# Gate blocks transposed by VectorE in 32x32 squares, and a convolution moved behind the rotation

## The chip, the cores and the metric

One core of a Trainium2 chip runs the whole program. The metric is device time in microseconds for one execution; lower is better.

## The reference

A trunk of two layers on 256 tokens of width 2048, in float32. Layer 0 computes retention and a gated linear recurrence (RG-LRU) side by side from one input projection; layer 1 is sliding-window attention; a squared-ReLU MLP of width 8192 follows each. What the change touches is the recurrent block:

```
q, k, v, g, xb, gate = split(h @ w_in)
xc = conv_b + sum over taps of xp[:, tap:tap+S] * conv_w[tap]      # 4 taps along the tokens
r = sigmoid(xc @ w_a + b_a);  i = sigmoid(xc @ w_x + b_x)          # per block of 128 channels
a = exp(-8 r softplus(-lam));  b = sqrt(1 - a^2) * i * xc
h = scan(a, b);  lru_out = h * gelu(gate)                          # tanh form of gelu
q, k = rotary(q), rotary(k)                                        # for the retention part
```

## The kernel before, in words

The kernel streams weights. Each projection is cut into **blocks** of 512 output columns; there are 89 of them, and each has a **slot** (numbered from 0) on TensorE. Slots 0 to 11 are the blocks of `MIX_IN`: xb, gate, q, k, v, g for the first half of the channels, then the same for the second. A slot is eight **halves**, k = 0 to 7. Each half multiplies 256 rows of weights with 256 tokens. A float32 product is made from three: each operand is split into a high part and a low part, so a half is 12 matmuls (lines 1127 to 1129).

ScalarE writes the high part of a half's weights (`cut_hi`, line 579), VectorE subtracts to get the low part (`cut_lo`, line 788). Both work four halves ahead (`AHEAD`), in a ring of four (`RING`), so at step k of slot b they cut half k + 4. TensorE starts a half when its low part is there, and ScalarE may cut into a ring place when TensorE has left it. SyncE loads 1 MB of weights as soon as two halves of the unit that lay in its place are cut.

Each engine runs the same double loop over slots and steps. In every step VectorE does, in this order: what block b - 1 needs (`post`), the retention's step, the recurrent block's steps (`lru`), the attention's step, and last the cut. An instruction waits on the engine for its semaphores, and everything written behind it waits too.

What `post` does for a finished block b - 1 in slot b: ScalarE scales it out of PSUM to `stage` at step 0 (`leave`, line 629). An xb block is transposed by VectorE in 16 instructions of 32x256 (`turn_quadrants`, line 983), spread over steps 1, 2 and 3 by `QUADRANTS_AT`. A gate block is transposed by TensorE in eight matmuls with the identity (`turn_block`, line 1158) after half 2, and copied from PSUM to `gate_t` by VectorE at step 3 (line 1031). A q or k block is rotated by VectorE at step 1 (`rotate`, lines 833 to 838), transposed by TensorE after half 4, and copied at step 5.

The recurrent block has eight channel groups n = 0 to 7. `LRU_IN_SLOT` gives them slots 2, 3, 4, 5, 8, 9, 10 and 11; `lru(n, step)` runs with step = k in that slot, and step = 8 + k in the next. VectorE makes the convolution at step 2 (line 865 and three times line 868), TensorE the gate matmuls after half 4 (`lru_gates`, lines 1191 and 1192, behind a wait on `conv_done`), ScalarE the sigmoids, exponential, tanh and root at steps 5 to 7, and VectorE the scan at step 8. At step 9 ScalarE writes the high part of h and VectorE the low part (line 893). TensorE waits for these low parts in slot 12 (`LRU_BEFORE`). GpSimd computes the polynomial and product of gelu (lines 553 to 557), once the gate block is transposed and the group before is done. In slot 1, at step 6, VectorE also runs the softplus of the decay parameters, 14 small instructions.

Of the kernel before, what the change touches and what calls it, by code (L numbers as in the profile page):

```python
# [45 lines left out]
LG = LRU_BLOCKS // 2  # L46
TAPS = 4
# [22 lines left out]
def mlp_blocks(last_kind):  # L70
    blocks = []
    for c in range(CHUNKS):
# [15 lines left out]
NORM_OF = [0] * MIX_OUT0 + [None] * COLS + [1] * 32 + [2] * (1 + KV) + [None] * COLS + [3] * 32  # L88
BY_ACT = {"xb", "gate", "q", "k", "v", "g", "kv", "aq", "up"}
TURNED = {"xb", "gate", "q", "k", "g", "kv", "aq", "up", "res"}  # L90
DIRECT = {"xb", "kv"}
BY_QUADRANT = {"up", "res"} | DIRECT
SPLIT = {"g", "up", "res"}
PLAIN = TURNED - SPLIT - DIRECT
FROM_STAGE = {"gate", "aq"}

TURN_AT = {"aq": 0, "q": 4, "k": 4, "g": 4, "gate": 2}

QUADRANTS_AT = {kind: {1: 4, 2: 6, 3: 6} for kind in BY_QUADRANT}
STATIONARY_STARTS = ({MIX_OUT0, MLP0, QKV0, ATT_OUT0, MLP1}  # L100
                     | {m + PERIOD * c + COLS for m in (MLP0, MLP1) for c in range(CHUNKS)})

# [16 lines left out]
def late(b):  # L119


    return 2 if b in WOVEN else 0
# [3 lines left out]


LRU_BEFORE = {2: 4, 4: 6, 5: 8}


def lru_steps(b, k):
# [7 lines left out]
def total(kinds, each):  # L139

    out = [0]
    for kind, _ in BLOCKS:
        out.append(out[-1] + (each if kind in kinds else 0))
    return out
# [7 lines left out]
N_TURNED = total(TURNED, 2)  # L152
N_MOVED = total(TURNED - DIRECT, 2)
N_SPLIT = total(SPLIT, 2)


def out_at(kind, b):

    return (max(QUADRANTS_AT[kind]) if kind in BY_QUADRANT else TURN_AT[kind]) + 1 + late(b)

# [66 lines left out]
def build(nc, t):  # L227
    ctx = ExitStack()
    with ctx:
# [33 lines left out]
        def take(*shape):  # L263
            n = int(np.prod(shape))
            at = place["at"]
            place["at"] = at + n
            assert place["at"] <= AREA, (place["at"], AREA)
            v = area[:, at:at + n]
            if len(shape) == 2:
                v = v.rearrange("p (a b) -> p a b", a=shape[0])  # L270
            if len(shape) == 3:
                v = v.rearrange("p (a b c) -> p a b c", a=shape[0], b=shape[1])
            return v
# [3 lines left out]
        xb_t = take(LG, TAPS - 1 + SEQ)  # L277
        gate_t = take(LG, SEQ)
        q_t = take(HG, SEQ)
        k_t = take(HG, SEQ)  # L280
# [15 lines left out]
        kk_t = take(KV, SEQ)  # L296
        qq_t = take(PAIRS, SEQ)
# [96 lines left out]
        def vec(c):  # L394
            return vecs[:, c:c + 1]
# [170 lines left out]
        def _(act):  # L566
# [39 lines left out]
            def leave(slot, kind, j):  # L606

                b = slot.b - 1
                act.wait_ge(half_used, slot.halves(late(b)))
                if b > 0 and BLOCKS[b - 1][0] in DIRECT:  # L610

# [161 lines left out]
        def _(dve):  # L773
            links = [0]

            def link(ins):

                links[0] += 1
                ins.then_inc(chain, 1)
                dve.wait_ge(chain, links[0])  # L780
# [79 lines left out]

            def lru(n, step):
                xb = xb_t[:, n % LG, :]
                if step == 2:

                    link(nc.vector.tensor_scalar(xc[:, :], xb[:, 0:SEQ], vec(V_CONV + n), vec(V_CB + n),
                                                 ALU.mult, ALU.add))
                    for tap in range(1, TAPS):
                        ins = nc.vector.scalar_tensor_tensor(  # L868
                            xc[:, :], xb[:, tap:tap + SEQ], vec(V_CONV + LRU_BLOCKS * tap + n), xc[:, :],
                            ALU.mult, ALU.add)  # L870
                        if tap < TAPS - 1:
                            link(ins)
                    ins.then_inc(conv_done, 1)
                if step == 6:

                    dve.wait_ge(th_done, n + 1)
                    nc.vector.tensor_scalar(th[:, :], th[:, :], 2.0 ** -116, None, ALU.max).then_inc(th_safe, 1)
                if step == 8:

                    dve.wait_ge(sig_done, 2 * n + 2)  # L880
                    link(nc.vector.tensor_tensor(xc[:, :], xc[:, :], ri[:, 1, :], ALU.mult))
                    dve.wait_ge(root_done, n + 1)
                    link(nc.vector.scalar_tensor_tensor(th[:, :], a_lru[:, :], 1.0, th[:, :], ALU.add, ALU.mult))
                    link(nc.vector.memset(th[:, 0:1], 1.0))
                    link(nc.vector.tensor_tensor(xc[:, :], xc[:, :], th[:, :], ALU.mult))
                    if n > 0:
                        dve.wait_ge(lru_hi, n)
                    link(nc.vector.tensor_tensor_scan(h_lru[:, :], a_lru[:, :], xc[:, :], 0.0, ALU.mult, ALU.add))
                    dve.wait_ge(gelu_done, n + 1)
                    nc.vector.tensor_tensor(h_lru[:, :], h_lru[:, :], gel2[:, :], ALU.mult).then_inc(lru_done, 1)  # L890
                if step == 9:
                    dve.wait_ge(lru_hi, n + 1)
                    nc.vector.tensor_tensor(b_lo[:, 8 + n, :], h_lru[:, :], b_hi[:, 8 + n, :].bitcast(F32),
                                            ALU.subtract).then_inc(lru_lo, 1)
# [63 lines left out]
            def turn_quadrants(slot, k, kind, j):  # L958


                at = {tick + late(slot.b - 1): n for tick, n in QUADRANTS_AT[kind].items()}
                if k not in at:
                    return
                if k == min(at):

                    dve.wait_ge(turned_out, slot.count(N_TURNED, -1, INIT_HALVES))
                if k == min(at) and kind == "up":
                    dve.wait_ge(squared, slot.count(N_SQUARED, 0))
                if k == min(at) and kind == "res":
                    dve.wait_ge(evac_dve, slot.count(N_EVAC_DVE, 0))  # L970
                if k == min(at) and kind in DIRECT:
                    dve.wait_ge(evac_act, slot.count(N_EVAC_ACT, 0))
                src = x[:, :, j * NB:(j + 1) * NB] if kind == "res" else stage
                src = src.rearrange("p t (k f c) -> p t k f c", k=COLS, f=QUADRANTS)
                if kind in DIRECT:
                    tile = {"xb": xb_t[:, :, TAPS - 1:], "kv": kk_t}[kind]
                    dst = tile.rearrange("p k (t a c) -> p t k a c", t=TT, a=QUADRANTS)
                else:
                    dst = turn.rearrange("p m (k t a c) -> p t (m k) a c", k=2, t=TT, a=QUADRANTS)
                done = sum(n for tick, n in at.items() if tick < k)  # L980
                for n in range(done, done + at[k]):
                    a, f = divmod(n, QUADRANTS)
                    ins = nc.vector.transpose(dst[f * QUAD:(f + 1) * QUAD, :, :, a, :],  # L983
                                              src[a * QUAD:(a + 1) * QUAD, :, :, f, :])
                if k == max(at):
                    ins.then_inc(turned_out if kind in DIRECT else turned, 2)

            def plain_target(kind, j):
                tile = {"gate": gate_t, "q": q_t, "k": k_t, "aq": qq_t}[kind]
                return lambda m: tile[:, 2 * m:2 * m + 2, :]  # L990

            def post(slot, k):
# [28 lines left out]
                if kind in BY_QUADRANT:  # L1021
                    turn_quadrants(slot, k, kind, j)
# [91 lines left out]
        def _(pe):  # L1114
# [48 lines left out]
            def post(slot):  # L1163
# [3 lines left out]
                if kind not in TURNED - BY_QUADRANT:  # L1167
                    return
                if kind in FROM_STAGE:
                    pe.wait_ge(evac_act, slot.count(N_EVAC_ACT, 0))  # L1170
# [122 lines left out]
            def body(slot):  # L1293
                b = slot.b
                if b >= 2:
# [3 lines left out]
                    else:  # L1299
                        pe.wait_ge(evac_dve, slot.count(N_EVAC_DVE, -1))  # L1300
                if b in STATIONARY_STARTS:
                    pe.wait_ge(turned_out, slot.count(N_TURNED, -1, INIT_HALVES))
                for k in range(HALVES):
                    if b == 0:
                        pe.wait_ge(turned_out, k + 1)
                    if b == MIX_OUT0 and k in LRU_BEFORE:
                        pe.wait_ge(lru_lo, LRU_BEFORE[k])
                    if b == ATT_OUT0 and k == 0:
# [3 lines left out]
                    if b in WOVEN and k == HALVES - 2:  # L1312
# [3 lines left out]
                        else:  # L1316
                            pe.wait_ge(evac_dve, slot.count(N_EVAC_DVE, 0))
                    if b - 1 in STATIONARY_STARTS and k == 0:
                        pe.wait_ge(turned_out, slot.count(N_TURNED, -1, INIT_HALVES))
# [19 lines left out]
                    if b > 0:  # L1339
                        kind, j = BLOCKS[b - 1]  # L1340
                        if kind in TURN_AT and k == TURN_AT[kind] + late(b - 1):
                            post(slot)
# [33 lines left out]
```

## Time and profile before

| | us |
|---|---|
| median of 3 runs (2016.01 to 2016.54) | 2016.15 |
| the profiled execution | 2016.07 |
| its span, first to last instruction | 2014.3 |
| TensorE matmul busy | 2003.6 |
| VectorE busy | 1438.7 |
| ScalarE busy | 1019.9 |
| GpSimd busy | 45.2 |

The span belongs to the profiled execution; the rest of its 2016.07 us lies outside the first and the last instruction. PE is TensorE's matmul, PEld its weight load, DVE is VectorE, ACT is ScalarE, POOL is GpSimd. A matmul is listed at some 0.39 us though the next starts 0.23 us after it, since they are pipelined: differences of start times give the pace.

### The profile page before, as it was taken

The numbers are of one execution on the slowest core, as the hardware profiler recorded it, in microseconds if no ns is written. First come the engines' busy times: TensorE is split into PE (matmuls) and PEld (weight loads), VectorE is DVE, ScalarE is ACT, GpSimd is POOL, SyncE is SP. The second block draws the span as 40 slices with busy tenths as digits, with TensorE's granted clock in tenths as the row PEclk, the third lists the DMA queues.
The fourth block names the chain that finished last, engine by engine and source line by source line (L and its number), as shares of the span: only waits on it lengthen the run. The fifth ranks groups of instructions, "written<-read, shape, count | busy, mean of one in ns | idle before, by whom it ended". The sixth has DMA issues, their size and how long they took to land.

```text
span 2014.3 us, 24679 instructions
## 1 busy us (share of the span) xinstructions
PE 2003.6 (99%) x9187; PEld 1655.2 (82%) x9187; DVE 1438.7 (71%) x1975; ACT 1019.9 (51%) x1345; POOL 45.2 (2%) x55
## 2 busy tenths in 40 slices
PE   9999999999999999999999999999999999999998
PEld 7888888888888888888888877888888888888886
DVE  6777778987558657846888777978548756854875
ACT  6665665455345435434545555555435434544554
POOL 1110110000000000000000000000000000000000
PEclk9999999999999999999999999999999999999999
DMA  8556556556566656565656535566565656565563
GB/s 303 186 170 213 169 167 209 189 187 210 189 188 197 199 188 189 197 197 176 202 187 200 174 129 167 186 193 202 192 191 190 202 188 187 187 208 188 188 202 112
DMA packets 191437, 382.50 MB, mean 190 GB/s; under 512 B 6264, under 2 KB 7040, under 8 KB 191232
## 3 DMA queue, kind: packets, MB, share of 16 engines
q1 hardware_dynamic: 190112, 377.58, 57.7%
q0 software_dynamic: 1216, 3.88, 0.6%
q8 instruction: 49, 0.80, 0.2%
q14 instruction: 28, 0.23, 0.0%
q10 hardware_dynamic: 32, 0.01, 0.0%
HBM read 379.34 MB, written 2.10 MB: 189 GB/s over the span
## 4 chain that ended last, share of the span: by engine, by line
PE 95%; DVE 3%; ACT 2%; issue 0%; ACTq 0%
PE acc L1127 31%; PE acc L1129 30%; PE acc L1128 30%; ACT w_hi L579 1%; DVE w_lo L788 1%; PE bank L1158 0%; PE bank L1237 0%; PE bank L1261 0%; PE bank L1247 0%; DVE area L868 0%; PE acc L1278 0%; ACT L648 0%; ACT L654 0%; DVE turn L835 0%; PE bank L1191 0%
## 5 line engine op out<-in xcount | busy, mean ns | idle before, releaser
L788 DVE TENSOR_TENSOR w_lo<-raw,w_hi 128x1024 fp32r<-128x1024 f32 x712 | 865.5, 1225 | 520.2 <-ACT w_hi L579 517.4
L579 ACT ACTIVATE w_hi<-raw 128x1024 fp32r<-128x1024 f32 x712 | 748.1, 1059 | 809.0 <-PE acc L1129 805.6
L1127 PE MATMUL acc<-w_hi,a_hi 128*128 128x512 f32 x1568 | 614.6, 392 | 0.0
L1129 PE MATMUL acc<-w_hi,a_lo 128*128 128x512 f32 x1568 | 610.4, 389 | 0.0
L1128 PE MATMUL acc<-w_lo,a_hi 128*128 128x512 f32 x1568 | 610.3, 389 | 0.0
L1127 PE MATMUL acc<-w_hi,b_hi 128*128 128x512 f32 x1264 | 492.4, 390 | 0.0
L1129 PE MATMUL acc<-w_hi,b_lo 128*128 128x512 f32 x1264 | 491.8, 389 | 0.0
L1128 PE MATMUL acc<-w_lo,b_hi 128*128 128x512 f32 x1264 | 491.8, 389 | 0.0
L1127 PEld LDWEIGHTS acc<-w_hi,a_hi 128*128 128x128 f32 x1568 | 294.4, 188 | 62.6 <-issue 1.8
L1129 PEld LDWEIGHTS acc<-w_hi,a_lo 128*128 128x128 f32 x1568 | 294.3, 188 | 61.7
L1128 PEld LDWEIGHTS acc<-w_lo,a_hi 128*128 128x128 f32 x1568 | 294.4, 188 | 60.2
L1127 PEld LDWEIGHTS acc<-w_hi,b_hi 128*128 128x128 f32 x1264 | 237.2, 188 | 49.7 <-issue 0.7
L1129 PEld LDWEIGHTS acc<-w_hi,b_lo 128*128 128x128 f32 x1264 | 237.2, 188 | 49.4
L1128 PEld LDWEIGHTS acc<-w_lo,b_hi 128*128 128x128 f32 x1264 | 237.3, 188 | 49.2
L983 DVE STREAM_TRANSPOSE turn<-stage 32x256 f32<-32x256 f32 x512 | 223.1, 436 | 7.7
L587 ACT ACTIVATE b_hi<-turn 128x512 fp32r<-128x512 f32 x64 | 36.9, 625 | 107.2 <-DVE turn L983 107.2
L983 DVE STREAM_TRANSPOSE turn<-x 32x256 f32<-32x256 f32 x192 | 83.6, 436 | 2.9
L629 ACT ACTIVATE stage<-acc,rinv 128x512 f32<-128x512 f32 x92 | 57.6, 674 | 1.4 <-DVE rinv L821 1.4
L1001 DVE TENSOR_TENSOR x<-x,acc 128x512 f32<-128x512 f32 x78 | 49.8, 681 | 0.0
L796 DVE TENSOR_TENSOR b_lo<-turn,b_hi 128x512 fp32r<-128x512 f32 x64 | 41.2, 685 | 0.0
L634 ACT ACTIVATE stage<-stage 128x512 f32<-128x512 f32 x64 | 36.7, 626 | 0.0
L589 ACT ACTIVATE a_hi<-turn,vecs 128x256 fp32r<-128x256 f32 x24 | 12.1, 503 | 35.7 <-DVE turn L983 35.7
(171 smaller groups left out, 587.1 us busy)
## 6 DMA issues: line engine op xcount, KB each, us to landing
raw<-in_mlp_w_up SPq DMA_DIRECT2D x128, 1024.0 KB, 5.5
raw<-in_mlp_w_down SPq DMA_DIRECT2D x128, 1024.0 KB, 5.1
raw<-in_hyb_w_in SPq DMA_DIRECT2D x44, 1024.0 KB, 5.2
raw<-in_attn_w_qkv SPq DMA_DIRECT2D x20, 1024.0 KB, 5.1
raw<-in_hyb_w_out SPq DMA_DIRECT2D x16, 1024.0 KB, 5.2
raw<-in_attn_w_out SPq DMA_DIRECT2D x16, 1024.0 KB, 5.1
raw<-in_hyb_w_in SPq DMA_DIRECT2D x8, 512.0 KB, 9.9
out_y<-x SPq DMA_DIRECT2D x4, 512.0 KB, 3.0
```

The source lines that it names most:

```text
L579: nc.scalar.activation(w_hi[:, h % RING], raw[:, h // 2, 2 * (h % 2):2 * (h % 2) + 2, :], ACT.Copy).then_inc(hi_ready, 1)
L587: nc.scalar.activation(hi[:, kt:kt + 2, :], src, ACT.Copy).then_inc(turned_hi, 1)
L589: nc.scalar.activation(hi[:, kt, :], src[:, 0, :], ACT.Copy, scale=vec(scale))
L629: ins = nc.scalar.activation(stage[:, tt, :], src, ACT.Relu if kind == "up" else ACT.Copy, scale=s)
L634: nc.scalar.activation(stage[:, tt, :], stage[:, tt, :], ACT.Square).then_inc(squared, 1)
L788: nc.vector.tensor_tensor(w_lo[:, h % RING], raw[:, h // 2, 2 * (h % 2):2 * (h % 2) + 2, :], w_hi[:, h % RING].bitcast(F32), ALU.subtract) ...
L796: nc.vector.tensor_tensor(lo[:, kt:kt + 2, :], src, hi[:, kt:kt + 2, :].bitcast(F32), ALU.subtract).then_inc(turned_out, 1)
L983: ins = nc.vector.transpose(dst[f * QUAD:(f + 1) * QUAD, :, :, a, :], src[a * QUAD:(a + 1) * QUAD, :, :, f, :])
L1001: nc.vector.tensor_tensor(xs, xs, acc[:, b % 2, tt, :], ALU.add).then_inc(evac_dve, 1)
L1127: nc.tensor.matmul(a, xh, wh, start=first, stop=False)
L1128: nc.tensor.matmul(a, xh, wl, start=False, stop=False)
L1129: ins = nc.tensor.matmul(a, xl, wh, start=False, stop=last)
```

## The change

Gate blocks join the blocks that VectorE transposes straight to their place (`DIRECT`): six transposes at step 0 and ten at step 1 of the slot. TensorE's transposes and VectorE's copies for them go. The convolution runs at step `CONV_AT[n % 4]`: at step 1 for n = 1, 2, 5 and 6 (the slots of q and k, behind the rotation), and at step 2 for the others, as before. The low part of h is written at step 10 in place of step 9.

```
-DIRECT = {"xb", "kv"}
+DIRECT = {"xb", "kv", "gate"}
 BY_QUADRANT = {"up", "res"} | DIRECT
 SPLIT = {"g", "up", "res"}
 PLAIN = TURNED - SPLIT - DIRECT
-FROM_STAGE = {"gate", "aq"}
-
-TURN_AT = {"aq": 0, "q": 4, "k": 4, "g": 4, "gate": 2}
+FROM_STAGE = {"aq"}
+
+TURN_AT = {"aq": 0, "q": 4, "k": 4, "g": 4}
 
 QUADRANTS_AT = {kind: {1: 4, 2: 6, 3: 6} for kind in BY_QUADRANT}
+QUADRANTS_AT["gate"] = {0: 6, 1: 10}
...
+CONV_AT = [2, 1, 1, 2]
...
-                if step == 2:
+                if step == CONV_AT[n % LG]:
...
-                if step == 9:
+                if step == 10:
                     dve.wait_ge(lru_hi, n + 1)
...
-                    tile = {"xb": xb_t[:, :, TAPS - 1:], "kv": kk_t}[kind]
+                    tile = {"xb": xb_t[:, :, TAPS - 1:], "gate": gate_t, "kv": kk_t}[kind]
...
-                tile = {"gate": gate_t, "q": q_t, "k": k_t, "aq": qq_t}[kind]
+                tile = {"q": q_t, "k": k_t, "aq": qq_t}[kind]
```

The step 10 shown is VectorE's; ScalarE's high part stays at step 9.

## Rows read from the trace of the kernel before

**Rows 1.** The page: the chain that ended last, by engine; a weight load's time to landing.

```profile
PE 95%; DVE 3%; ACT 2%; issue 0%; ACTq 0%
...
raw<-in_hyb_w_in SPq DMA_DIRECT2D x44, 1024.0 KB, 5.2
```

**Rows 2.** Waits of TensorE: waiting line, releaser, us in total, times, longest.

```profile
PE acc L1278 <- DVE junk L1042: 1.5, 1, 1.5
PE bank L1191 <- DVE area L868: 1.2, 4, 0.3
```

**Rows 3.** Timeline, TensorE, slot 3: start us, us, instruction, count, idle before.

```profile
92.99 1.03 PE L1158 MATMUL bank<-ident,turn 128*128 128x128 f32 x8
94.34 0.70 PE L1191 MATMUL bank<-area 128*128 128x256 f32 x2 [0.32 <-DVE area L868]
...
95.55 0.40 PE L1128 MATMUL acc<-w_lo,a_hi 128*128 128x512 f32 x1
```

**Rows 4.** Timeline, VectorE, slot 3, behind the rotation.

```profile
90.84 0.42 DVE L893 TENSOR_TENSOR b_lo<-area,b_hi 128x256 fp32r<-128x256 f32 x1
91.18 1.22 DVE L788 TENSOR_TENSOR w_lo<-raw,w_hi 128x1024 fp32r<-128x1024 f32 x1
...
92.76 1.53 DVE L868 SCALAR_TENSOR_TENSOR area<-area,vecs 128x256 f32<-128x256 f32 x3
```

**Rows 5.** Timeline, TensorE, slot 2: the gate block's transposes, then the gate matmuls.

```profile
64.00 1.03 PE L1158 MATMUL bank<-ident,stage 128*128 128x128 f32 x8
...
65.10 0.39 PE L1128 MATMUL acc<-w_lo,a_hi 128*128 128x512 f32 x1
...
70.35 0.60 PE L1191 MATMUL bank<-area 128*128 128x256 f32 x2
...
71.45 0.40 PE L1128 MATMUL acc<-w_lo,a_hi 128*128 128x512 f32 x1
```

**Rows 6.** Timeline, VectorE, slot 2, from the end of softplus.

```profile
59.85 4.62 DVE L788 TENSOR_TENSOR w_lo<-raw,w_hi 128x1024 fp32r<-128x1024 f32 x4
64.39 0.41 DVE L865 TENSOR_SCALAR area<-area,vecs 128x256 f32<-128x256 f32 x1
64.84 1.53 DVE L868 SCALAR_TENSOR_TENSOR area<-area,vecs 128x256 f32<-128x256 f32 x3
...
67.42 1.28 DVE L1031 COPY area<-bank 128x512 f32<-128x512 f32 x2
```

**Rows 7.** Timeline, VectorE, slot 1: six transposes of the xb block.

```profile
44.76 2.68 DVE L983 STREAM_TRANSPOSE area<-stage 32x256 f32<-32x256 f32 x6
```

**Rows 8.** Timeline, ScalarE: evacuation of the gate block, slots 2 and 8.

```profile
58.61 1.25 ACT L629 ACTIVATE stage<-acc,rinv 128x512 f32<-128x512 f32 x2
...
201.24 1.25 ACT L629 ACTIVATE stage<-acc,rinv 128x512 f32<-128x512 f32 x2
```

**Rows 9.** Timeline, TensorE, slot 8: the second ordinary matmul behind the gate matmuls.

```profile
215.71 0.40 PE L1128 MATMUL acc<-w_lo,a_hi 128*128 128x512 f32 x1
```

**Rows 10.** Timeline, VectorE, slot 8: two of the cuts.

```profile
206.81 1.23 DVE L788 TENSOR_TENSOR w_lo<-raw,w_hi 128x1024 fp32r<-128x1024 f32 x1 [1.43 <-ACT w_hi L579]
...
213.17 1.34 DVE L788 TENSOR_TENSOR w_lo<-raw,w_hi 128x1024 fp32r<-128x1024 f32 x1 [0.92 <-ACT w_hi L579]
```

**Rows 11.** Groups by line, VectorE, 79.1 to 103 us: busy us, mean ns, idle.

```profile
L835 DVE TENSOR_TENSOR turn<-stage,rope 128x512 f32<-128x512 f32 x1 | 1.2, 1226 | 0.0
L833 DVE TENSOR_TENSOR turn<-stage,rope 128x512 f32<-128x512 f32 x1 | 1.1, 1105 | 0.0
L834 DVE TENSOR_TENSOR area<-stage,rope 128x512 f32<-128x512 f32 x1 | 0.9, 880 | 0.0
...
L836 DVE TENSOR_TENSOR area<-stage,rope 128x512 f32<-128x512 f32 x1 | 0.7, 678 | 0.0
```

**Rows 12.** Timeline, GpSimd, slot 3, beside the rotation.

```profile
85.04 1.46 POOL L553 TENSOR_TENSOR area<-area 128x256 f32<-128x256 f32 x1 [10.09 <-DVE area L890]
```

**Rows 13.** The page: TensorE's granted clock in 40 slices, in tenths.

```profile
PEclk9999999999999999999999999999999999999999
```

## The prediction

> **What bounds the kernel now.** I read the page first. TensorE's busy time fills the span but for 11 us, and the chain that ended last lies on it for 95%; VectorE has 3% of that chain, ScalarE 2% [rows 1]. The list of waits says who holds TensorE up: its one wait of any size on another engine, after the start, is line 1191, the gate matmuls of the recurrent block, on line 868, the convolution, 4 times [rows 2]. So time can be won where TensorE gets less work or where those four waits go, and lost where VectorE becomes later than TensorE. Everything else is cover. A slot is eight halves of 12 matmuls. From the second matmul of half 3 to the gate matmuls are 23 matmuls in 5.25 us, or 0.228 each, 2.73 a half [rows 5]. I number slots from 0, as the code does; slot b also does the leftovers of block b-1.
>
> The four waits lie in slots 3, 4, 9 and 10, where q and k blocks are rotated. In slot 3 the block transposes start at 92.99 and the second ordinary matmul behind the gates at 95.55: 2.56 us [rows 3]. Unhindered, eight transposes cost 0.87 (64.00 to 65.10 is 1.10, less one matmul step of 0.23), and the four gate matmuls also cost 0.87 (70.35 to 71.45, less the same) [rows 5]. Together with the step that is 1.97, so the wait is worth 0.59. I found 2.54 in the other three slots, which is 0.57 each: 2.3 us in all.
>
> **The change part by part.**
>
> The eight TensorE transposes of a gate block go, in slots 2 and 8: 0.87 each [rows 5]. The two copies from PSUM go as well, 1.28 us of VectorE, but they stand behind the convolution, at 67.42 [rows 6], so they shorten nothing that anybody waits for.
>
> Sixteen VectorE transposes of 32x256 come in their place, six at step 0 and ten at step 1. Six of the same shape took 2.68 us [rows 7], so one is 0.447 and sixteen are 7.15 us. All of them stand in front of the convolution, which runs at step 2, and its result is what the gate matmuls after half 4 wait for. Queued behind them are also the cuts of halves 4 and 5.
>
> Slot 2. VectorE comes into this slot late: the small softplus instructions end just before 59.85, and from there on it works without a gap: four cuts (1.14 from start to start), then the convolution, done at 64.84 + 1.53 = 66.37 [rows 6]. The evacuation that the new transposes wait for ends at 58.61 + 1.25 = 59.86 [rows 8], before VectorE gets to them (two cuts after 59.85), so nothing of the 7.15 is hidden ahead: the convolution ends at 73.52. Without its own transposes TensorE would want it at 70.35 - 0.87 = 69.48. The slack of today, some 4 us, is smaller than the work put into it. The cut of half 4 does fit: 59.85 + 3 cuts of 1.14 + 2.68 = 65.95, and half 4 starts at 64.00 + 2.73 = 66.7.
>
> GpSimd is a second term. It works out the gelu polynomial as soon as the gate block is there. Today that falls beside one cut; now it falls beside the last cut and the convolution. What this costs VectorE has rows: under GpSimd's three instructions, the first of them 1.46 us long [rows 12], the rotation's lines 833, 834 and 835 took 1.105, 0.880 and 1.226, and line 836, the same kind and size, 0.678 when GpSimd had finished [rows 11]: 0.43 + 0.20 + 0.55 = 1.2, less one overlap of starts, 1.1. At the low end stands the cut at 213.17, which took 1.34 in place of 1.23, or 0.1 more [rows 10]; at the high end I put the length of GpSimd's longest instruction, 1.5. I take 1.1, since the rotation is nearest: VectorE instructions with two operands in SBUF right behind a cut.
>
> So the convolution ends at 74.6, the gate matmuls start 0.05 later (92.76 + 1.53 to 94.34 in slot 3 [rows 3, 4]), and the second ordinary matmul 1.21 later still, as behind a wait in slot 3 [rows 3]: 75.9 against 71.45, a loss of **4.4 us** with the saved 0.87 already in it. TensorE idles about 5.2 us there.
>
> Slot 8. No softplus here: VectorE waits for ScalarE's cuts (1.43 us idle before 206.81 [rows 10]). The evacuation ends at 201.24 + 1.25 = 202.49 [rows 8]. Then 16 transposes 7.15, two cuts 2.28, the convolution 1.98 (64.39 to 66.37 [rows 6]) and 0.05 to start: 213.95; with 1.1 for GpSimd 215.05. Plus 0.05 and 1.21: 216.3 against 215.71 [rows 9], a loss of **0.6 us**. Without GpSimd's part it would be a gain of 0.5.
>
> A rule stands against this part, in sentences that the sum does without. The rows have 0.87 us of TensorE against 7.15 us of VectorE for the same block. The Trainium skill, "VectorE: DVE Perf Modes", section "Rules for kernel authors", sends a 128x128 transpose to TensorE if a PSUM destination is fine, and keeps VectorE's for 32x32. With both engines idle enough, the rows would give a gain of 1.7 us for two blocks; with VectorE on the path, as the rows have it in slot 2, the rule's advice is right.
>
> The convolution ahead of the cut, slots 3, 4, 9 and 10. Today the order is rotation, the low part of h (0.34 from start to start), cut of half 5 (1.14 [rows 6]), convolution [rows 4]. The new order is rotation, convolution, cut, low part. The convolution is done 1.48 us earlier, and 0.59 was the wait. What is late next is the cut of half 5: it ends 0.34 before the old end of the convolution, at 93.95. TensorE, unhindered, starts the gates at 92.99 + 0.87 = 93.86 and half 5 about 0.68 later, at 94.5 [rows 3, 5]. So 0.6 us of margin, and the wait goes entirely: **-2.3 us**. This also holds after the wait in the slot before, since ScalarE's and VectorE's work for the recurrent block hangs on the end of half 5 there.
>
> The low part moved to step 10 has one other reader, TensorE in slot 12, which wants the last of them before its half 5. It moves behind one cut of 1.14; a half is 2.73. Cost nothing. In slots 5 and 11 it only comes later than the cut. Weight loads are held by the cuts: the one that the cut of half 5 in slot 2 releases goes out 7.15 us later, at about 71.5. ScalarE wants it at the start of slot 3, about 82 by today's times and 86 by the new ones, and a load lands in 5.2 us [rows 1]. Nothing.
>
> Sum: 4.4 + 0.6 - 2.3 = **+2.7 us**. The profiled execution took 2016.07 in all (span 2014.3), 0.08 under the median of the runs; it becomes 2018.8, and the median **2018.9 us**. With 0.1 for GpSimd in each slot it is +0.7, with 1.5 it is +3.5: 2016.8 to 2019.7.
>
> **The rivals.**
>
> Slower: TensorE's clock falls in the new idle stretch of slot 2. Against it: the granted clock stands at nine tenths or more in all 40 slices [rows 13]. For it: TensorE's longest idle stretch is 1.5 us, at the very start [rows 2], so the trace says nothing of one of 5 us. The two levels are 2.4 and 1.2 GHz; at the lower one a half's 12 matmuls take up to 2.73 us more. I price one half: 2018.9 + 2.7 = 2021.6, two would give 2024.3. [...] The Trainium skill, "TensorE: Matmul & The Clock Gate", section "What's actually happening", says that the clock is throttled by default and that idleness brings the lower level back; no row here shows it.
>
> Faster: the gate transposes are covered after all, because VectorE is less late in slot 2 than I read. Then both blocks give their 0.87, and the q and k slots their 2.3: -4.0, 2012.1. Against it is the unbroken run of VectorE from 59.85 [rows 6]; it would need 4 us of slack more than the rows have.
>
> The q and k waits stay: the cut behind the convolution becomes the late one. GpSimd's work can still fall beside the convolution there, and costs up to 1.1; the wait begins where the cut slips by 0.6 and has eaten the gain at 1.2. Then the 2.3 are not won: +5.0, 2021.2.
>
> **How the numbers follow.** Forecast 0.62, clock 0.22, no cover problem 0.06, q and k gain lost 0.10. A measurement of this kernel can tell 0.2%, 4 us, from no change: 2012.1 to 2020.2. Slower gets the clock's 0.22, 0.07 of the lost gain (the rest of it is won in part and stays inside) and 0.02 of the forecast: 0.31. Faster gets 0.05 of the covered case. The rest is same: 0.64. The range runs from 2016.3 to 2022.0: it leaves out the covered case and a clock that costs two halves.
>
> **What would show it.** Right: one wait of TensorE at line 1191 on line 868 of about 5 us in slot 2 and of about 1 in slot 8, none in slots 3, 4, 9 and 10; sixteen transposes between cuts in slots 2 and 8; the convolution's lines stretched by GpSimd. Wrong: a wait at line 1191 in slot 2 under 3 us, a granted clock under 1 around 75 us, or waits at line 1127 on the cuts in the q and k slots.

## The result, and the profile after

The changed kernel takes 2023.41 us (median of 7 runs, 2022.2 to 2023.72), the kernel before 2016.15 (2016.01 to 2016.54). The ratio is 1.0034, 95% interval 1.0024 to 1.0044: slower by 7.3 us, and outside the predicted range, which ended at 2022.0. The profiled execution took 2023.7 with a span of 2021.9, against 2016.07 and 2014.3.

The waits of TensorE, whole run (waiting line, releaser, us in total, times, longest). Lines after the diff are three higher than before: 1194 was 1191, 871 was 868, 791 was 788, 1132 was 1129.

```profile
PE bank L1194 <- DVE area L871: 6.0, 2, 4.9
PE acc L1281 <- DVE junk L1045: 1.5, 1, 1.5
PE bank L1161 <- DMA x<-in_x: 1.2, 1, 1.2
PE acc L1132 <- issue: 0.8, 2, 0.4
```

Against [rows 2], the gate matmuls wait for the convolution twice, not four times, and one of the two waits is of 4.9 us. Two lines are new: a wait on the load of x at the start, and two stops in an ordinary matmul line for which the profile names nobody ("issue").

VectorE in slot 2 (timeline: start us, us, instruction, count), to be laid beside [rows 6]. All times here have 1.3 us of a later start in them:

```profile
61.18 2.35 DVE L791 TENSOR_TENSOR w_lo<-raw,w_hi 128x1024 fp32r<-128x1024 f32 x2
63.45 2.67 DVE L986 STREAM_TRANSPOSE area<-stage 32x256 f32<-32x256 f32 x6
66.14 1.23 DVE L791 TENSOR_TENSOR w_lo<-raw,w_hi 128x1024 fp32r<-128x1024 f32 x1
67.39 4.49 DVE L986 STREAM_TRANSPOSE area<-stage 32x256 f32<-32x256 f32 x10
71.91 1.23 DVE L791 TENSOR_TENSOR w_lo<-raw,w_hi 128x1024 fp32r<-128x1024 f32 x1
73.05 0.70 DVE L868 TENSOR_SCALAR area<-area,vecs 128x256 f32<-128x256 f32 x1
73.79 1.98 DVE L871 SCALAR_TENSOR_TENSOR area<-area,vecs 128x256 f32<-128x256 f32 x3
```

No gap anywhere, sixteen transposes ahead of the convolution, and the convolution itself stretched from 0.41 and 1.53 to 0.70 and 1.98. TensorE at that place, to be laid beside [rows 5]:

```profile
75.82 1.20 PE L1194 MATMUL bank<-area 128*128 128x256 f32 x2 [4.89 <-DVE area L871]
76.81 1.06 PE L1195 MATMUL bank<-area 128*128 128x256 f32 x2
77.31 0.99 PE L1130 MATMUL acc<-w_hi,a_hi 128*128 128x512 f32 x1
78.10 0.63 PE L1131 MATMUL acc<-w_lo,a_hi 128*128 128x512 f32 x1
78.53 0.63 PE L1132 MATMUL acc<-w_hi,a_lo 128*128 128x512 f32 x1
78.95 0.56 PE L1130 MATMUL acc<-w_hi,a_hi 128*128 128x512 f32 x1
79.34 0.40 PE L1131 MATMUL acc<-w_lo,a_hi 128*128 128x512 f32 x1
79.58 0.40 PE L1132 MATMUL acc<-w_hi,a_lo 128*128 128x512 f32 x1
```

Behind the idle 4.89 us the matmuls start 0.43 us apart, and from 79.34 on again 0.23 apart. That is TensorE's clock. Three stretches of the windows view (us, PE busy, granted clock, share of DMA, GB/s) have it at 0.66 on average in the second, between its two levels of 2.4 and 1.2 GHz:

```profile
70.00:75.00 5.00, 0.93 (x5) 1.00 0.16 14
75.00:80.00 5.00, 4.18 (x11) 0.66 0.66 221
80.00:85.00 5.00, 5.00 (x23) 1.00 0.60 196
```

In slot 3 the transposes and the gate matmuls now follow each other without a gap, where [rows 3] have one:

```profile
100.22 1.03 PE L1161 MATMUL bank<-ident,turn 128*128 128x128 f32 x8
101.09 0.60 PE L1194 MATMUL bank<-area 128*128 128x256 f32 x2
```

Slot 8 has a wait of 1.14, and far behind, in the loop over the MLP of layer 0, TensorE stops in the second and in the third turn of the loop:

```profile
221.10 0.70 PE L1194 MATMUL bank<-area 128*128 128x256 f32 x2 [1.14 <-DVE area L871]
...
592.50 0.39 PE L1131 MATMUL acc<-w_lo,a_hi 128*128 128x512 f32 x1
593.28 0.50 PE L1132 MATMUL acc<-w_hi,a_lo 128*128 128x512 f32 x1 [0.40 <-issue]
```

The next matmul should start at 592.73; it starts at 593.28. The weight-load view has the same stop at 0.82 us, a second one at 768, and a shorter one some four us ahead of each (589.43 and 764.52). The shorter ones stand at the first matmul of slots 25 and 33, that is at the first matmul of the loop's second and third turn; the longer ones come 14 matmuls later. (The profile puts the shorter ones down to a cut of VectorE, but by the kernel's order that half's cut lies four halves, some 11 us, back.) The page says what the queue of program code moved in the whole run; after first, before second (queue: packets, MB, share):

```profile
q8 instruction: 66, 1.08, 0.2%
```

```profile
q8 instruction: 49, 0.80, 0.2%
```

Seventeen more packets of program code. The list of DMA queues for a stretch says where they lie. The loop's second and third turn, after (590 to 939 us) first and before (584 to 931 us) second:

```profile
q1 hardware_dynamic: 33573, 66.66, 58.1%
q8 instruction: 17, 0.28, 0.3%
```

```profile
q1 hardware_dynamic: 33645, 66.81, 60.0%
```

Before, no code moves in these two turns: the second line is missing, for 347 us. After, all seventeen packets lie there, nine in the second turn and eight in the third. So in the changed kernel the code of the loop was fetched again in each of these turns, and in the kernel before it was not.

The difference of 7.6 us in the spans, by the start of the same matmul in both traces (the second ordinary one behind the gate matmuls or the transposes):

| stretch | before | after | lost in it |
|---|---|---|---|
| slot 0, half 6 | 28.81 | 30.11 | +1.3 |
| slot 2, to the gates | 71.45 | 78.10 | +5.35, 1.07 of it clock |
| slot 3 | 95.55 | 102.19 | 0.0: clock +0.57, q -0.58 |
| slot 4 | 119.65 | 125.72 | -0.57 |
| slot 8 | 215.71 | 222.30 | +0.5 |
| slots 9 and 10 | 263.89 | 269.41 | -1.07 |
| to slot 12 | 314.62 | 320.13 | 0.0 |
| the rest of the span | 2014.3 | 2021.9 | +2.1, all of it at the start of the loop's second and third turn |

So 4.3 + 0.5 for VectorE's lateness, -2.2 for the four waits, 1.6 for the clock, 2.1 for the loop and 1.3 at the start, 7.6 in all.

### The profile page after: what moved, and what is told of

Same layout as the page of the kernel before. It is cut to its first block, busy times and chain, and to the rows that moved or that the text cites. A ratio compares the mean times of both kernels' runs of the same rounds, so it can differ in the third digit from the quotient of the medians.

```text
span 2021.9 us, 24663 instructions
## 1 busy us (share of the span) xinstructions
PE 2004.4 (99%) x9171; PEld 1654.2 (82%) x9171; DVE 1450.0 (72%) x2003; ACT 1020.1 (50%) x1345; POOL 46.5 (2%) x55
## 4 chain that ended last, share of the span: by engine, by line
PE 95%; DVE 2%; ACT 1%; issue 1%; DMA 0%; SPq 0%; ACTq 0%
PE acc L1130 31%; PE acc L1132 31%; PE acc L1131 31%; DVE area L986 1%; DVE w_lo L791 1%; ACT w_hi L582 0%; PE bank L1161 0%; PE bank L1240 0%; PE bank L1264 0%; PE bank L1250 0%; DMA x<-in_x 0%; PE bank L1194 0%; DVE area L871 0%; PE bank L1195 0%; ACT junk L602 0%
## 5 line engine op out<-in xcount | busy, mean ns | idle before, releaser
L986 DVE STREAM_TRANSPOSE area<-stage 32x256 f32<-32x256 f32 x80 | 34.9, 436 | 1.2
```

## The experiments

All medians have the kernel before on the same chip beside them; it gave 2016.04 to 2016.39.

**The changed kernel once more.**

> The changed kernel once more, for a second trace. Its first trace had four losses against before: 1.3 us at the start (TensorE waited for the second load of x), 4.3 us of wait in slot 2, 1.6 us of lowered clock behind that wait, and 2.1 us in the MLP loop of layer 0, where TensorE stood still at 589 and 764 us. If the start is chance, its 1.3 us can be absent here and the time lies anywhere from 2022.2 to 2023.7. If the clock and the loop belong to the kernel, both come again with the same sizes. If they were chance too, this run can fall to about 2019.7.

2022.67 us (1.0031, 1.0019 to 1.0043). The start cost 0.6 here (29.42 against 28.81) where it cost 1.3 in the first trace of the same program, so its size varies by chance: in this trace and those of the other kernels below the same matmul lies between 28.41 and 29.61, for programs of which most do the same up to there. The clock fell again, at a cost of 2.2 us here (1.1 in the gate matmuls, 1.1 in five behind them), and the stops in the loop came again, with 66 packets. So the wait in slot 2, the lowered clock and the stops belong to the changed kernel; the size of the clock's part (1.6 and 2.2) and of the start's (1.3 and 0.6) differs from one execution to the next.

**The gate part alone.**

```diff
-CONV_AT = [2, 1, 1, 2]
+CONV_AT = [2, 2, 2, 2]
-                if step == 10:
+                if step == 9:
```

> The gate blocks by VectorE as in the change, but convolution at step 2 in all slots and the low part at step 9, as before. Theory (the loss is all the gate part's, the convolution's move won 2.3 us): the four waits of 0.57 come back in slots 3, 4, 9, 10, slot 2 loses 4.3 + 1.6, slot 8 loses 0.5, the loop 2.1, the start 0 to 1.3: 8.5 to 9.8 us over before, 2024.7 to 2026.0. Rival (the convolution's new place is what hurts, for instance by a later cut of half 5): about 2016 to 2019, below the changed kernel.

2026.26 us (1.0048, 1.0034 to 1.0062), 3.6 above the changed kernel beside it. Six waits at line 1194 now, the two long ones and the four old ones. The convolution's move is a gain inside the change. Up to slot 12, the start left out, this trace has lost 7.3 us against before and the first trace of the changed kernel 4.2. Of the 3.1 between them 0.9 is the clock, which came back four matmuls later here (2.5 us in place of 1.6); the other 2.2 are the four waits.

**The convolution's move alone**, on the kernel before.

```diff
+CONV_AT = [2, 1, 1, 2]
-                if step == 2:
+                if step == CONV_AT[n % LG]:
-                if step == 9:
+                if step == 10:
```

> Only the convolution behind the rotation and the low part at step 10; gate blocks as before. Theory: the four waits go and nothing else moves, TensorE's program has the same length, so no stops in the loop either: 2016.15 - 2.3 = 2013.9. Rival (the cut of half 5 becomes the late one): 2016.1. Rival (the stops in the loop come from any change of VectorE's order): 2016.0.

2013.81 us, 0.999 (0.9981 to 0.9999). Its waits of TensorE, the whole list:

```profile
PE acc L1280 <- DVE junk L1044: 1.5, 1, 1.5
PE bank L1160 <- DMA x<-in_x: 1.1, 1, 1.1
```

None at the gate matmuls, 49 packets, no stop in the loop. The -2.3 of the prediction is -2.2 in the trace (from 28.81 to 314.62 before, 29.28 to 312.87 here), and both rivals fall.

**Softplus moved to the end of slot 2.**

```diff
-                    if slot.i is None and b == 1 and k == 6:
+                    if slot.i is None and b == 2 and k == 4:
```

(on ScalarE and on VectorE)

> The changed kernel with the softplus of the decay parameters (VectorE's 14 small instructions and ScalarE's exponential) at step 4 of slot 2 in place of step 6 of slot 1, which is behind the convolution. Theory (the wait of slot 2 is there because softplus makes VectorE 5 us late): the wait of 5 us goes, with it the lowered clock; left are -0.87 in slot 2, +0.5 in slot 8, -2.3 in the q and k slots, +2.1 in the loop, 0 to 1.3 at the start: 2015.6 to 2016.9. Rival (softplus does not matter, the 16 transposes alone are too much for the slot): slot 2 keeps 2 us or more of wait and the time stays above 2018.

2024.41 us (1.0039, 1.0025 to 1.0052): 7.5 above the expected range. Slot 2 did what the theory said: the wait there shrank to 1.5, and the clock did not fall in it. The loss came back in slot 3. ScalarE had to wait for VectorE's first softplus instructions (timeline; in brackets the idle time before):

```profile
74.46 1.28 ACT L747 ACT_TABLE_LOAD   x1 [5.74 <-DVE soft L849]
```

Behind this line on ScalarE stand a cut and the sigmoids, so the whole chain of the recurrent block was late by the time of the rotation, and TensorE waited first for a cut (0.62 us at 93.43) and then for the rotation. The clock fell behind this second wait, though it is of 1.89 us only: the eight transposes behind it took 1.95 us where [rows 3] and the changed kernel have about 1.03 (timeline, then windows with the columns as above):

```profile
98.33 1.95 PE L1161 MATMUL bank<-ident,turn 128*128 128x128 f32 x8 [1.89 <-DVE turn L841]
```

```profile
98.00:100.00 2.00, 1.67 (x8) 0.60 0.00 0
```

The run shows that ScalarE, too, has no room there, and that this was the wrong place, not that softplus is innocent.

**Softplus moved to slot 0**, `b == 0 and k == 6` in both places.

> The changed kernel with softplus at step 6 of slot 0, where VectorE waits about 1.1 us before every cut, in place of step 6 of slot 1. (At step 4 of slot 2 it only moved the loss to slot 3: ScalarE stood 5.7 us in front of its exponential and so cut late.) Theory (the wait of slot 2 is softplus's lateness plus 1.5 us): slot 2 becomes like slot 8, +0.5 where it was +4.3, the clock stays up there; q and k -2.3, slot 8 +0.5, loop +2.1, start 0 to 1.3: 2017.0 to 2018.3. Rival (slots 0 and 1 have no room for softplus): a new wait there on the cuts and 2020 or more.

2019.34 us (1.0015, 1.0006 to 1.0024), 3.3 under the changed kernel. The expected 2017.0 to 2018.3 was missed by a new wait. TensorE's weight loads, 30 to 62 us, then 62 to 100:

```profile
PEld acc L1130 <- DVE w_lo L791: 2.6, 2, 1.4
```

```profile
PEld bank L1194 <- DVE area L871: 1.6, 1, 1.6
```

In slot 2, 1.6 us are left of the 5.3 that the same view has in the changed kernel, the clock stays at 1.00, and slot 1 now waits 2.6 us for its cuts. So about 3.7 us of the long wait were softplus's lateness; the transposes alone, on an engine that is on time, cost what they cost in slot 8.

**The same with the convolution first.**

```diff
-CONV_AT = [2, 1, 1, 2]
+CONV_AT = [0, 1, 1, 2]
```

> As softplus_early, and the convolution of slots 2 and 8 at step 0, behind six of the transposes, ahead of the other ten and of GpSimd's work. Theory: no wait at the gate matmuls in any slot, so each gate block gives its 0.87: -1.7 - 2.3 + 2.1 (loop) + 0 to 1.3 (start): 2014.2 to 2015.5. Rival (the cut of half 5 behind 16 transposes becomes the late one): a wait at line 1130 on line 791 in slots 2 and 8, 0.5 us or more each, 2015.5 to 2017.

2016.74 us, 1.0003 (0.9994 to 1.0012). No wait at the gate matmuls in any slot, so each gate block gives its 0.87: from slot 6 to the gates of slot 8 it took 44.44 us here and 45.34 before, and slot 2 gains 0.9 in the same way. The 2.6 us of slot 1 and the loop's stops eat the gain, and the first of these is why the time missed its range.

**TensorE's program filled up to its old length.** In front of the gate matmuls of slot 2:

```diff
+                if n == 0:
+                    for i in range(16):
+                        nc.tensor.transpose(bank[:, i // 8, (i % 4) * P:(i % 4 + 1) * P],
+                                            x[:, i % 2, (i % 4) * P:(i % 4 + 1) * P], ident[:, :])
```

> The changed kernel with 16 transposes of x into two free banks, whose result nobody reads, in front of the gate matmuls of slot 2, inside TensorE's wait: TensorE's program has again as many instructions as before. Theory (the stops at 589 and 764 us come from where the loop lies in TensorE's program): both go and with them 2.1 us, and the instruction queue moves 49 packets, not 66. If in addition the lowered clock hangs on the idle time, it has 3.1 us of it here in place of 4.9: the clock stays up or falls for less, another 0 to 1.6. Together 2019.0 to 2020.8. Rival (the stops come from VectorE's longer program, or from chance): 66 packets and 2021 to 2023.

2020.46 us (1.0021, 1.0012 to 1.003), 2.2 to 3 under the changed kernel. 49 packets, and no stop at an ordinary matmul line. VectorE's program is the changed kernel's to the instruction, so the stops follow TensorE's, and the rival, VectorE's longer program, falls. The transposes shortened the idle stretch to 3.10, and the clock fell all the same, though only some 1.3 us after TensorE had begun again: the gate matmuls still took the 0.70 us of [rows 3], and the slow pace begins at 76.08.

```profile
74.54 0.70 PE L1198 MATMUL bank<-area 128*128 128x256 f32 x2 [3.10 <-DVE area L871]
...
76.50 0.63 PE L1130 MATMUL acc<-w_hi,a_hi 128*128 128x512 f32 x1
```

```profile
75.00:80.00 5.00, 5.00 (x17) 0.66 0.65 222
```

**GpSimd kept off the convolution** of slots 2 and 8.

```diff
+                if n % LG == 0:
+                    pool.wait_ge(conv_done, n + 1)
```

> The changed kernel, but GpSimd begins the gelu polynomial of slots 2 and 8 only when the convolution there is done. Theory (GpSimd costs the convolution 0.7 to 0.8 us, since lines 868 and 871 took 0.70 and 1.98 where they took 0.41 and 1.53 before): they take 0.41 and 1.53 again, and each wait is 0.8 us shorter: 1.6 in all, and a further 0 to 1.6 if the shorter wait of slot 2 keeps the clock up: 2019.5 to 2021.1. Rival (the longer times have nothing to do with GpSimd): as the changed kernel, 2022.7.

2021.83 us (1.0029, 1.0018 to 1.0039). The convolution took its old 0.41 and 1.53:

```profile
71.72 0.41 DVE L870 TENSOR_SCALAR area<-area,vecs 128x256 f32<-128x256 f32 x1
72.17 1.53 DVE L873 SCALAR_TENSOR_TENSOR area<-area,vecs 128x256 f32<-128x256 f32 x3
```

The two waits came to 4.5 in place of 6.0, and the clock fell behind 4.14 us too. So GpSimd's share is shown, 0.7 us in each slot where I had 1.1. Against the second set of runs of the changed kernel the time fell by 0.8, less than the 1.6 hoped for: gelu came late instead. ScalarE stood 2.6 us in front of it in slot 8, and slot 9 took 23.89 us from gates to gates where the changed kernel took 23.55.

**The transposes behind the convolution**, softplus in its old place.

```diff
-QUADRANTS_AT["gate"] = {0: 6, 1: 10}
+QUADRANTS_AT["gate"] = {1: 4, 2: 6, 3: 6}
-CONV_AT = [2, 1, 1, 2]
+CONV_AT = [0, 1, 1, 2]
```

> The changed kernel with softplus in its old place (at step 6 of slot 0 it made slot 1's cuts late, 2.6 us), the convolution of slots 2 and 8 at step 0, and the gate block's 16 transposes behind it, four, six and six at steps 1, 2 and 3. Theory (only what stands ahead of the convolution and of the cuts of halves 4 and 5 costs): conv ends at about 64.1, cuts 4 and 5 at 65.2 and 68.2 where TensorE wants them at 66.7 and 70.3; no wait in slots 2 and 8, no lowered clock; -1.7 - 2.3 + 2.1 for the loop + 0 to 1.3 at the start: 2014.2 to 2015.5. Rival (later cuts, 7 in slot 2 above all, or the gelu in slot 3, become late): 2016 or more.

2021.53 us (1.0028, 1.0018 to 1.0039). Slots 2 and 8 do as forecast, with no wait at their gate matmuls. The rival came true: the gelu is late, and with it slots 3 and 9. From the trace of the next kernel, the same but for its start (timeline of ScalarE, slot 2):

```profile
78.76 0.42 ACT L647 ACTIVATE area<-area 128x256 f32<-128x256 f32 x1 [5.81 <-POOL area L558]
```

The sigmoid of gelu waits 5.81 us for GpSimd, which waits for the last transpose, and ScalarE's cuts stand behind it. In this kernel and the next, TensorE waits 0.64 us for a cut at 91 us and then 1.84 us for the rotation of slot 3, and the clock falls here too (0.52 over 96 to 98 us). In the next kernel it fell only behind a third wait, of 0.80 us for the convolution: the eight transposes between the two took 1.09. So in this kernel the transposes may be neither ahead of the convolution nor much behind it.

**The same, TensorE's program filled up** by other means:

```diff
-                for _ in range(n):
-                    ins = nc.tensor.matmul(acc[:, 1, 1, 0:SEQ], junk[:, 0:P], junk[:, 0:SEQ], start=True, stop=True)
+                for _ in range(2 * n):
+                    ins = nc.tensor.matmul(acc[:, 1, 1, 0:P], junk[:, 0:P], junk[:, 0:P], start=True, stop=True)
```

> As spread, and the eight warming matmuls at the start, 256 columns each, written as sixteen of 128: the same columns, and TensorE's program again as long as before. Theory (the loop's stops come from the length of TensorE's program ahead of it): no stops at 589 and 764 us, 49 packets on the instruction queue: 2012.1 to 2013.4, under the kernel before and under the one with the convolution's move alone. Rival (the padding worked in pe_pad for another reason): 66 packets and the time of spread.

2019.91 us (1.0017, 1.0008 to 1.0026): 1.6 under the kernel above, 49 packets, no stops. The time expected, 2012.1 to 2013.4, was missed by 6.5; it rested on the same wrong idea about gelu as the one before. The part on the loop holds, in a second way.

**That filling alone**, on the kernel before.

> The kernel before with the sixteen short warming matmuls alone, so that TensorE's program is longer than before by what the change had taken from it. If only a shorter program brings the stops: 49 packets and 2016.1. If each position of the loop has its own cost, the packets can differ, with 0 to some 3 us more. The start may move by some tenths.

2016.10 us, 1.0 (0.9991 to 1.0009), 49 packets, no stops. A longer program costs nothing here; only the shorter one did.

**What the runs leave standing**: the convolution's move; the gate block of slot 2 by TensorE, only that of slot 8 by VectorE, with its convolution at step 0; the short warming matmuls.

```diff
-          ("xb", 1), ("gate", 1), ("q", 1), ("k", 1), ("v", 1), ("g", 1)]
+          ("xb", 1), ("gd", 1), ("q", 1), ("k", 1), ("v", 1), ("g", 1)]
-DIRECT = {"xb", "kv"}
+DIRECT = {"xb", "kv", "gd"}
+QUADRANTS_AT["gd"] = {0: 6, 1: 10}
+CONV_AT = [2, 1, 1, 2, 0, 1, 1, 2]
```

> What the runs so far leave standing: the convolution behind the rotation in the q and k slots, the gate block of slot 2 by TensorE as before, only the one of slot 8 by VectorE (six transposes, the convolution at step 0, ten transposes), and the warming matmuls in halves, so that TensorE's program is 8 instructions longer than before and not 8 shorter. Theory: -2.3 for q and k (conv_only gave 2013.8), -0.9 for the transposes of slot 8, no wait in any of these slots, 49 packets: 2012.9. In spread, gelu came late because the transposes ended at step 3; here they end at step 1, as in early_conv_first, where slot 8 won its 0.9. Rival (the loop's stops come back with another length of the program): 66 packets and 2015.

2012.97 us, ratio 0.9984 (0.9975 to 0.9993): 3.1 us under the kernel before, where 3.2 were expected, and 10 under the changed one. VectorE in slot 8:

```profile
201.47 2.67 DVE L986 STREAM_TRANSPOSE area<-stage 32x256 f32<-32x256 f32 x6
204.16 0.41 DVE L868 TENSOR_SCALAR area<-area,vecs 128x256 f32<-128x256 f32 x1
204.61 1.53 DVE L871 SCALAR_TENSOR_TENSOR area<-area,vecs 128x256 f32<-128x256 f32 x3
206.05 1.22 DVE L791 TENSOR_TENSOR w_lo<-raw,w_hi 128x1024 fp32r<-128x1024 f32 x1
207.30 4.50 DVE L986 STREAM_TRANSPOSE area<-stage 32x256 f32<-32x256 f32 x10
```

The convolution is done at 206.1, and TensorE takes it up at 212.56 without a wait.

## Why the prediction was wrong, step by step

The waits were forecast well. The step that failed is the sum, which took the waits and the work taken off TensorE for the whole effect. It put at nothing what TensorE loses after a long wait (the clock, kept outside the sum as a rival; measured 1.6 us) and what a shorter program of TensorE does to the loop behind it (in no part at all; measured 2.1 us). With the measured waits and the clock alone the time would be 2016.15 + 2.6 + 1.6 = 2020.4, inside the range; it left the range with the loop and the start.

- **The transposes go from TensorE, -0.87 each.** Right where no wait hid it: 0.9 in slot 8 of early_conv_first and of the last kernel.
- **Slot 2, +4.4.** Right in cause and size: +4.3 without the clock, sixteen transposes 7.15 long, an unbroken VectorE, idle 4.9 where 5.2 was said. The closeness is luck in part: GpSimd's term was 0.7, not 1.1, while the transposes and the two cuts between them took 9.60 us where the terms give 9.43. The evacuation and the cut of half 4 did fit. Softplus as the cause of the lateness is shown by moving it.
- **Slot 8, +0.6.** Measured +0.5.
- **The convolution behind the rotation, -2.3.** Measured -2.2, and in conv_only alone the same; the cut of half 5 did not become late.
- **The low part at step 10, nothing.** Right.
- **Sum of these:** 4.3 + 0.5 - 2.2 = +2.6 against a forecast of +2.7. What was left out is larger than what was in.
- **The clock** stood as a rival with a chance of 0.22 and a price of 2.7 us for one half. The list of signs named it too, a granted clock under 1 around 75 us, and it came: 0.66. It fell in all five traces with an idle stretch of 3.1 to 4.9 us in slot 2 and cost 1.6 to 2.5 us, 1.6 in the profiled run. The likeliest case should have contained it: the forecast itself put 5.2 us of idleness there, more than three times the longest in the trace. The price of a whole half, 2.7, was somewhat too high. The page that I cited for the rival, the Trainium skill's "TensorE: Matmul & The Clock Gate", section "What's actually happening", names this fall and the return; the trace agrees, with 0.43 us from start to start in place of 0.23.
- **The loop, +2.1**, was in no part of the prediction. I counted the matmuls that the change takes away as time only, not as length of the program. The trace of before has 49 packets of code and no stop, and nothing in it could have told me the size.
- **The start, +1.3 in the profiled run**, varies by chance: -0.4 to +1.3 against the trace of before, in the traces that I have. It was not in the range either; the first runs of the kernel before lie within 0.5 us, which I took for the spread of any program with the same start, while later ones of the same kernel lie between 2015.49 and 2018.67. Without it the sum is 2.6 + 1.6 + 2.1 = 6.3 us, and the medians differ by 7.3. The 1.0 between them is not taken apart: start and clock both vary, and an execution without a trace shows neither.

## What to carry to other kernels

Before work is moved to an engine that has idle time on average, read where that engine stands when the work arrives and who waits for what is queued behind it: VectorE was 71% busy, and still nearly 4 us late from softplus in the one slot that mattered, while in the other slot the same sixteen transposes were free once the convolution went ahead of them. When a sum holds a wait of TensorE longer than any in the trace, put the lowered clock into it as a term, not as a rival. A change in TensorE's instruction count ahead of a loop moved the loop's own time here: compare the code packets, turn by turn, and the stops for which nobody is named before a cause is sought in the edit, and try the same edit at the old length.

## What the runs showed of the hardware

- Idle stretches of TensorE of 3.10, 4.14, 4.89, 4.89 and 4.91 us were each followed by matmuls 0.43 us apart (granted clock 0.52 to 0.69 over 75 to 80 us), four to eight of them, and then by the old 0.23, at 1.6 to 2.5 us each time. Filling a part of the stretch with sixteen transposes did not prevent it. Behind the stretches of 3.10 and 4.14 us the gate matmuls still ran at the old pace, and the clock fell some 1.3 and 1.0 us after TensorE had begun again. In three traces it fell behind stretches of 1.84 (twice) and 1.89 us ahead of a rotation, each with one of 0.6 us some five us before it, and in one of the three only after a third, of 0.80. It did not fall behind those of 1.14 us in slot 8, of 1.15 and 1.55 us in slot 2 (the kernels with softplus moved), nor behind one of 1.7 us at the start (the changed kernel's second trace). Which property of the stretches decides was not tried.
- Sixteen matmuls and sixteen weight loads fewer ahead of the loop brought 17 more packets of 16 KB on the instruction queue and stops in two turns of layer 0's loop (in the weight-load view of the changed kernel 0.50 and 0.82 us in one, 0.46 and 0.84 in the other), none in layer 1's. All seventeen lie in the loop's second and third turn, where the kernel before fetched no code. This holds for all fourteen traces: 17 packets in these two turns and 2.0 to 2.4 us lost there in the eight with the shorter program, none and nothing in the other six. So the code of this loop can stay with TensorE from turn to turn, and with the shorter program ahead of it it did not. Both ways of writing as many instructions again removed the stops, and 16 matmuls more than before brought none. Why this length matters, and whether other lengths do, stays open; only these were tried (8 more, in the last kernel, brought none).
- GpSimd's three small instructions beside VectorE instructions with operands in SBUF stretched the convolution from 1.98 to 2.72 us.
- The second load of x at the start landed so that the same matmul began between 28.41 and 30.11 us in all the traces, with SyncE's first ten issues at the same times within 0.3 us in the two that I compared. What decides it was not tried.
